# Unread matrix products on TensorE before the expert stage of a two-layer backbone step

## The reference

```python
def expert_choice_ffn(h, w_router, w1, w3, w2):
    B, L, D = h.shape
    cap = EC_CAPACITY * L // N_EXPERTS
    aff = jax.nn.softmax((h @ w_router).astype(jnp.float32), axis=-1)
    gate, idx = lax.top_k(aff.transpose(0, 2, 1), cap)
    xs = jax.vmap(lambda hb, ib: hb[ib])(h, idx)
    a = jnp.einsum('becd,edf->becf', xs, w1)
    b = jnp.einsum('becd,edf->becf', xs, w3)
    y = jnp.einsum('becf,efd->becd', jax.nn.silu(a) * b, w2) * gate[..., None].astype(h.dtype)
    return jax.vmap(lambda yb, ib: jnp.zeros((L, D), yb.dtype).at[ib.reshape(-1)].add(yb.reshape(-1, D)))(y, idx)
```

## Time and profile before

| what | value |
|---|---|
| median of 3 executions | 2861.83 us |
| lowest and highest of them | 2856.95 and 2864.8 us |
| the profiled execution's own time | 2856.8 us |
| its span, first to last instruction | 2855.0 us |
| mean granted clock of TensorE, as a share of 2.4 GHz | 0.973 |
| TensorE busy with products | 2648.1 us, 93% of the span |
| VectorE / ScalarE / GpSimd busy | 51% / 27% / 25% |
| bytes moved by DMA | 608.13 MB |

### The profile page before, as it was taken

How to read it: one execution, slowest core, us unless ns; L and a number is a source line. 1 busy time by engine, 2 the same in 40 slices (tenths; PEclk the granted TensorE clock), 3 DMA queues, 4 the chain that set the end, 5 groups by cost and what they waited for, 6 DMA issues and landing times.

```text
span 2855.0 us, 71727 instructions
## 1 busy us (share of the span) xinstructions
PE 2648.1 (93%) x32240; PEld 2017.8 (71%) x32240; DVE 1445.9 (51%) x2057; ACT 779.3 (27%) x1182; POOL 707.7 (25%) x570
## 2 busy tenths in 40 slices
PE   7998999999996998999989999999999769989997
PEld 3655676666655998988856466766675569988885
DVE  4997334565435443333469863356643444333335
ACT  3113133443112223222221131343421213223232
POOL 2472223332101121111135623233130012111111
PEclk9998999999998999999999999999999989999999
DMA  8332311123228999999933322111132279999995
GB/s 338 129 125 88 110 54 70 51 73 133 88 112 305 400 394 406 406 406 403 357 148 118 125 89 92 68 58 65 67 133 118 89 287 402 395 402 405 406 414 192
DMA packets 56795, 608.13 MB, mean 213 GB/s; under 512 B 6592, under 2 KB 6720, under 8 KB 21344
## 3 DMA queue, kind: packets, MB, share of 16 engines
q1 hardware_dynamic: 42656, 555.76, 48.9%
q0 software_dynamic: 7168, 23.47, 3.3%
q10 hardware_dynamic: 6848, 27.27, 2.4%
HBM read 577.25 MB, written 29.23 MB: 212 GB/s over the span
## 4 chain that ended last, share of the span: by engine, by line
PE 55%; DMA 23%; DVE 16%; ACT 3%; issue 2%; DVEq 0%; POOL 0%; ACTq 0%; SPq 0%; POOLq 0%
PE ps L500 39%; DMA hT<-in_w_exp 22%; DVE region_b L1774 7%; PE ps L671 6%; PE ps L923 3%; DVE ring L2093 2%; ACT ring L1657 2%; PE ps L889 1%; PE ps L872 1%; PE ps L860 1%; DVE sig L1744 1%; DMA region_b<-h_rows,rstd 1%; PE ps L1216 1%; PE ps L1035 0%; DVE region_r L2052 0%
## 5 line engine op out<-in xcount | busy, mean ns | idle before, releaser
L500 PE MATMUL ps<-region_r,ring 128*64 128x80 f32 x24192 | 900.2, 236 | 68.7 <-ACT ring L1657 43.7
L500 PEld LDWEIGHTS ps<-region_r,ring 128*64 128x64 f32 x24192 | 877.6, 139 | 91.8 <-issue 46.3
L500 PE MATMUL ps<-hT,ring 128*128 128x320 f32 (+2 forms) x1440 | 432.8, 443 | 8.2 <-ACT hT L1272 8.2
L500 PEld LDWEIGHTS ps<-hT,ring 128*128 128x128 f32 x1440 | 258.2, 192 | 145.3 <-issue 66.5
L1774 DVE SCALAR_TENSOR_TENSOR region_b<-region_b,params 128x655 f32<-128x655 f32 x240 | 276.3, 1151 | 8.5
L2093 DVE COPY ring<-region_b 128x4096 f32<-128x4096 f32 x66 | 152.8, 2316 | 217.6 <-issue 113.2
L2359 POOL COPY region_b<-region_r 80x512 f32<-80x512 f32 x64 | 46.9, 732 | 701.2 <-PE ps L1152 690.8
L500 PE MATMUL ps<-region_b,ring 128*128 128x320 f32 x560 | 182.5, 435 | 0.0
L1657 ACT ACTIVATE ring<-region_b 128x4096 f32<-128x4096 f32 x28 | 101.3, 3619 | 270.6 <-DMA region_b<-in_w_exp 254.1
L500 PE MATMUL ps<-ring 128*128 128x320 f32 x504 | 150.2, 434 | 0.0
L2093 DVE COPY ring<-region_x 128x4096 f32<-128x4096 f32 x32 | 74.0, 2313 | 130.1 <-issue 76.0
(11 more groups left out here) (302 smaller groups left out, 3747.7 us busy)
## 6 DMA issues: line engine op xcount, KB each, us to landing
region_b<-in_w_exp SPq DMA_DIRECT2D x90, 2048.0 KB, 18.9
hT<-in_w_exp SPq DMA_DIRECT2D x46, 2048.0 KB, 18.6
region_x<-in_w_exp SPq DMA_DIRECT2D x44, 2048.0 KB, 18.6
ring<-in_w_mix SPq DMA_DIRECT2D x39, 2048.0 KB, 7.9
ring<-in_w_pair SPq DMA_DIRECT2D x32, 1536.0 KB, 6.6
ring<-in_w_first SPq DMA_DIRECT2D x6, 2048.0 KB, 9.2
ring<-in_w_ada SPq DMA_DIRECT2D x4, 2048.0 KB, 8.7
x_store<-region_m ACTq DMA_DIRECT2D x2, 2560.0 KB, 10.4
```

Of the source, the lines that this page charges most:

```text
L500: ins = pe.matmul(*args, **kw)
```

## The change

It defines a helper behind the last `next_ada` step and calls it at two places:

```diff
@@ -1128,6 +1128,14 @@
                 turn_h2(4)
                 next_ada(("turn", 1), ("rows", 2), ("turn", 2), ("rows", 3), ("turn", 3))
 
+                def idle_products(n):
+
+                    if l == 0:
+                        pe.wait_ge(S["ada_part_in"], ADA_BLOCKS + ADA_EARLY[1])
+                    for _ in range(n):
+                        pe.matmul(PS[1][:, 1, :], ones, cosT, start=True, stop=True)
+
+                idle_products(0 if l == 0 else 7)
                 need("best_found", 1)
                 pe.transpose(PS[3][0:CAP, 0, 0:NE], best, ident[0:NE, 0:NE])
                 pe.transpose(PS[3][0:CAP, 0, NE:2 * NE], best_at, ident[0:NE, 0:NE]).then_inc(S["best_turned"], 1)
@@ -1193,6 +1201,7 @@
                         need("act_ready", i - 1)
                         expert_block(n + 2, turns, y_ps, act, "y_done")
 
+                idle_products(7)
                 turn_rows(0, 0)
                 turn_rows(1, 1)
                 expert_half(0, 0, 0, False)
```

## The result

The changed kernel is slower. Its median is 2864.92 us (2859.35 to 2869.47, 20 runs) against 2859.95 us for the kernel before (2856.08 to 2864.8, 20 runs). The ratio is 1.0016 with a 95% interval of 1.001 to 1.0022, which is 4.6 us of 2860. I had forecast 2861.4 us, 0.4 us less than before; with 20 runs the interval is narrow enough to say that the sign was wrong, though the change stays under 0.3%. The two executions that the profiler recorded, 2856.8 us before and 2859.75 us after, both lie under their medians, so the traces show 2.9 us of the loss.

What follows compares the result with a forecast made beforehand. TensorE held 55% of the chain and DMA 23%, with the weight stream unpaused in the expert stages; −0.1 + 0 − 0.3 = −0.4 us took the 2861.83 us median to 2861.4 us, range 2854.2 to 2868.1.

Steps and rivals of the forecast that it cites:

- The sum: Whole kernel: −0.1 us in layer 0, 0 and −0.3 us for layer 1's two batches, together −0.4 us.
- The weight stream has no pause there: Both expert stages, 896 to 1400 and 2316 to 2800 us: DMA share 1.01 at 403 and 402 GB/s.
- Price of a product: One 512-column float32 product on TensorE: 0.86 us, 0.17 more for the last; seven take 6.0 us warm, 12.0 at half clock.
- Layer 0: Seven products behind the small transposes run warm, clock holds, TensorE's gain of about 2.0 us stays hidden; term −0.1 us.
- Layer 1: First seven end before the picks, term 0; second seven leave 4.3 us idle, clock falls again, term −0.3 us.
- The term −0.4 us for both layers: Forecast change of the whole kernel's time, from −0.1, 0 and −0.3 us.
- The one on the slower side: Products delay layer 0's row transposes and layer 1's small transposes, a batch taking 12.0 us: +9.1 us, 2870.9; chance 0.05.
- The warm rival: Clock also holds into layer 1's first expert block: −2.6 us there, −2.7 us in all, 2859.1; chance 0.13.

Runs made afterwards that it cites:

- the aligned run: The changed kernel plus 43 one-column products in TensorE's layer 1 pause, so 256 instructions are added ahead of layer 1's expert loop; 0.9991 of before, median 2858.51 us.

## Why the prediction was wrong, point by point

**The sum had no term for the program text; that is the step that failed.** I costed 21 products as time on TensorE (−0.1, 0 and −0.3 us), and an instruction that lies in a pause as free, without a reason. The profile had the hint: in the kernel before, TensorE's first blocks in the expert stages have idle times with no releaser, 6.8 us in layer 0 and 2.1 in layer 1. I read TensorE's idle time there as waiting for the stream. I took them for covered, because the DMA share was 1.01. The text alone, without any product, measured 1.0014, some 4.0 us slower; with the text brought to 256 instructions the same products measured 0.9991.

**"The weight stream has no pause there"** was right of the kernel before and was no property of the stage. In layer 1 the stream starts when TensorE ends its first block, and it keeps its lead only while TensorE hands back slots in time. With 7.3 us of pauses and a slow block it fell to 352 GB/s. I never asked how much delay the stream can take.

**Price of a product**: right. Seven took 6.28 us warm, 6.0 and 0.17 forecast, and 7.16 us where they began cold.

**Layer 0**: the products ran warm, and the slot's load kept its place in front of the row transposes. Wrong was that the clock would hold into the first block. It lost it 0.5 us into the block, behind idle times of 1.30 and 0.70 us, each shorter than the 2.01 us that I had leaned on. Nothing hung on it.

**Layer 1**: the first batch ended in time, the pause was 4.31 us (4.3 forecast), the clock fell in it, and the block gained 0.25 us (0.3 forecast). The term −0.4 us for both layers agrees with the aligned run as far as it can be measured.

**Rivals.** The one on the slower side was the wrong mechanism: no batch came in the way of anything. The warm rival was right in its size: with eleven products the stream started 2.7 us earlier, against the 2.6 us that I gave it.

**Not settled.** The pauses are waits for instructions by three signs: the spacing of 256 instructions, the walk with the text, and the packets that land 1.2 to 1.6 us before TensorE goes on; no run changed the fetch alone. What decides when a packet starts, and so why the pauses add up to 7.3 us at one alignment and to 2 us at another, and to 7.3 and 4.8 us with the same text, is open. So are the 2.9 us that the changed kernel gained between the first rows of the two layers, 1405.5 us where before has 1408.4. Five kernels have products in layer 0 and no increments; they spent 1402.6 to 1408.0 us there. The six other runs, without products in layer 0, spent 1406.6 to 1412.3, so single executions hardly tell the two apart.

## What to carry to other kernels

An instruction that fits into a pause is not free where a long stretch of new text follows, as here with the weight stream at full rate: it shifts the text behind it. Before such a change is judged, run one of the same length in instructions that does nothing, and look for idle times without a releaser in the first pass over the code. Keeping TensorE warm pays only if the unread work reaches up to the awaited data, and if that block sets something that is on the path.

## What was not expected of the hardware

- Pauses inside a run of matmuls recur at the same place when 256 instructions are added, and stand within a record of where the instruction count puts them for 28, 56, 84, 128 and 228. Singly they were 0.16 to 2.73 us long in layer 1, and up to 4.03 us in layer 0.
- TensorE went on 1.2 to 1.6 us behind the end of a 16,384-byte packet on the instruction queue in 94 of 95 such pauses.
- A semaphore increment as an instruction of its own cost TensorE some 148 ns (25.41 us for 172).
- The indexed fetch of 80 rows took TensorE's wait from 7.93 to 13.13 us when three more block loads were issued before it, so an idle stretch of the DMA queues had a use.
- The clock fell after idle times of 1.30 and 0.70 us within 2 us of one another, while single pauses of 2.01 and 2.34 us had left it up.
